# One step more between scores and transposes in the attention loop of two mix phases

## The chip, the cores and the metric

The kernel runs on one core of a Trainium2 chip. The metric is the device time of one execution in microseconds, the median over the runs of a kernel. A profiled execution has a time of its own; its trace is counted from its own start.

## The reference

The reference is two blocks of two layers each on one sequence of 512 tokens with 1024 features. The change is in the first block, in the softmax attention of both of its layers (4 heads, 96 query and key features, causal):

```python
def attend_block(args):
    qi, bi = args
    s = jnp.einsum('bqhd,bkhd->bhqk', qi, k).astype(jnp.float32) * scale
    qpos = bi * Q_BLOCK + jnp.arange(Q_BLOCK)
    causal = kpos[None, :] <= qpos[:, None]
    s = jnp.where(causal[None, None], s, jnp.finfo(jnp.float32).min)
    p = jax.nn.softmax(s, axis=-1)
    return jnp.einsum('bhqk,bkhd->bqhd', p.astype(v.dtype), v)
```

Its result stands beside two other mixers of the layer, a gate (`sgu_mixer`, products of `w_spatial` with the value half) and a pool (`pool_mixer`, running means over 2, 4, 8 and 16 tokens, then a product with `w_pool`). All three are normalized, joined and multiplied by `w_out`. Everything else, the feed-forward layers, the convolution, the second attention and the other products with large weights, is not touched.

## The kernel before, in words

Each engine has one hand-written program; the engines meet only in semaphores, and each carries out its instructions in the order written. The large products run on TensorE (PE) in weight slabs of 1 MB. The sync engine loads a slab, GpSimd (POOL) splits it into a high and a low part (L407, L411), and TensorE multiplies three times (L469 to L471). Where a phase streams slabs, TensorE is the engine that all others follow.

A mix phase (function `mix` in each engine's program, two phases, one for each layer) ends with an attention loop that is short of such products. It has 16 steps r = 0 to 15: head r // 4, block r % 4 of 128 query tokens. Because of the causal mask step r works on 128, 256, 384 or 512 keys (its width). The stages of a step are:

- scores(r), TensorE, L806, into PSUM bank 4 or 5;
- mask(r), VectorE (DVE), L1688: adds the mask, takes the row maximum, writes the buffer `W[:, r % 3]` (named work), and then L1691, the bias for the exponential. In the trace mask is an instruction and a read of its accumulator;
- exp(r), ScalarE (ACT), L1191, in place, with the row sum;
- scale(r), VectorE, L1699 and L1700: the reciprocal of the sum and the product with it, in place;
- transposes(r), TensorE, L819: one block of 128 for each 128 keys, into bank 6 or 7;
- copy(r), ScalarE, L1200: out of PSUM into `pt1` (named probs_t).

After the four steps of head h TensorE makes values(h), L790, with the transposed probabilities as moving operand, and ScalarE copies the result out, here called head copy(h), L1223. All engines count one loop variable t. In iteration t TensorE makes scores(t), then whatever stands in `between[t]`, then transposes(t-2). VectorE makes mask(t), `between[t]`, scale(t-1). ScalarE makes exp(t), copy(t-2), `between[t]`.

The `between` pieces belong to the gate and the pool, and to weight tiles of the phase. They hang on t. On TensorE: input tiles at t = 1 and 2 (24 large matmuls each), gate products at 5 (L768), pool products at 11 (L779), token sums at 13 and 15 (L508). On VectorE: pool_input at 2 and 3 (L1630), the gate at 6 and 7 (L1634, L1637), gate_sum at 9 (L1332, L1335), pool_sum at 14. On ScalarE: gate squares at 8, at 12 the copies of the pool products out of PSUM (L1177, pool_scaled) and their squares, and at t = 16 the two square roots for the token norms (L987), ahead of which a table load stands. GpSimd in the same stretch splits a slab and then computes the running means of the pool (L437 to L449).

Behind the loop TensorE makes two `spread_norm` (L516) with norms that VectorE prepares out of ScalarE's square roots, then values(3), then the first products with `w_out` (L469). These wait for the low parts of gate and pool (L1675).

Of the kernel before, what the change touches and what calls it, by code (L numbers as in the profile page):

```python
# [28 lines left out]
ACT = mybir.ActivationFunctionType  # L29
ALU = mybir.AluOpType  # L30


P = 128
T = 512
# [14 lines left out]
TOK = T // P  # L49
# [106 lines left out]
def build(nc, a):  # L156

    ctx = ExitStack()
    with ctx:
# [18 lines left out]
        ident = sb("ident", [P, P])  # L178
        ones = sb("ones", [P, P])
        cols = sb("cols_sb", [P, N_COLUMNS])  # L180
        stat = sb("stat", [P, 24])
# [12 lines left out]
        with ExitStack() as s:  # L194
# [18 lines left out]
            diag = sb("diag_sb", [P, T], F32, s)  # L213
            pa = sb("window_a", [P, T + 16], F32, s)
            pb = sb("window_b", [P, T + 16], F32, s)
            nar = sb("token_cols", [P, 232], F32, s)
# [30 lines left out]
        with ExitStack() as s:  # L247
            W = sb("work", [P, 8, T], F32, s)
# [9 lines left out]
        ps = ctx.enter_context(nc.psum_tensor("psum", [P, 8, T], F32))  # L258
# [51 lines left out]
        probs_turned = sem("probs_turned")  # L310
# [155 lines left out]
        def _(pe):  # L466
# [218 lines left out]
            def mix(p):  # L685
                L = p.layer
# [7 lines left out]
                for c in range(TOK):  # L694
                    if c % 2 == 0:
                        take(p, 4 + c // 2)
                    out = ps[:, 4 + c // 2, (c % 2) * 256:(c % 2) * 256 + 256]
                    for k in range(8):
                        ha, la = xh[:, k, c * P:(c + 1) * P], xl[:, k, c * P:(c + 1) * P]
                        hb, lb = wh[:, s, k * 256:(k + 1) * 256], wl[:, s, k * 256:(k + 1) * 256]  # L700
                        last = triple(out, ha, la, hb, lb, k == 0, k == 7)
# [10 lines left out]
                for h in range(HEADS):  # L712
                    take(p, h % 2)
                    for kk in range(2):
                        last = triple(ps[:, h % 2, :], *blk(s, 2 * h + kk), lath[:, kk, :], latl[:, kk, :], kk == 0, kk == 1)
# [78 lines left out]


                steps = HEADS * TOK
                for t in range(steps + 2):
                    if t < steps:
                        h, i = divmod(t, TOK)
                        b = 4 + t % 2  # L800
                        if i == 0:
                            pe.wait_ge(head_ready, L * HEADS + h + 1)
                            fed = 7 - h % 2
                            pe.wait_ge(drained[fed], p.drain[fed] + (2 if fed == 7 else 4) + h // 2)
                        take(p, b)
                        pe.matmul(ps[:, b, 0:(i + 1) * P], qk1[0:QK_HEAD, 2 * h, i * P:(i + 1) * P],  # L806
                                  qk1[0:QK_HEAD, 2 * h + 1, 0:(i + 1) * P], start=True, stop=True).then_inc(scores_done, 1)
                    if t > TOK + 1 and t % TOK == 2:
                        values(t // TOK - 1)
                    if t in between:  # L810
                        between[t]()
                    if t >= 2:
                        r = t - 2
                        h, i = divmod(r, TOK)
                        b = 6 + r % 2
                        pe.wait_ge(probs_ready, L * steps + r + 1)
                        take(p, b)
                        for kb in range(i + 1):
                            last = pe.transpose(ps[:, b, kb * P:(kb + 1) * P], W[:, r % 3, kb * P:(kb + 1) * P], ident[:])  # L819
                        last.then_inc(probs_turned, 1)  # L820
                spread_norm(p, 2)
                spread_norm(p, 3)
# [14 lines left out]
                for m in range(4):  # L837
                    j = 6 + m // 2
                    for k in range(4):
                        if m == 0:  # L840
                            pe.wait_ge(split_low, split_base_mix(p) + 7 + k + 1)
                        last = triple(ps[:, m, :], *blk((s0 + j) % 2, 2 * k + m % 2), mix_high[k], mix_low[k], False, k == 3)
# [103 lines left out]
        def _(act):  # L946
            step = Chain(act, act_step)
# [178 lines left out]
            def mix(p):  # L1126
                L = p.layer
# [14 lines left out]
                for c in range(TOK):  # L1142
                    if c % 2 == 0:
                        act.wait_ge(*((tile_done, p.tile + 4) if c < 2 else (slab_done, p.slab + 3)))
                    ins = act.activation(W[:, 5, 0:256], ps[:, 4 + c // 2, (c % 2) * 256:(c % 2) * 256 + 256], ACT.Square,
                                         accum_out=nar[:, 64 + c:65 + c])
# [8 lines left out]
                for n in range(2 * HEADS):  # L1155
                    part, h = divmod(n, HEADS)
                    b = 2 * part + h % 2
# [25 lines left out]
                between = {8: gate_squares, 12: pool_scaled}  # L1183

                steps = HEADS * TOK
                for t in range(steps + 2):
                    if t < steps:
                        h, i = divmod(t, TOK)
                        n = (i + 1) * P
                        act.wait_ge(max_ready, L * steps + t + 1)  # L1190
                        act.activation(W[:, t % 3, 0:n], W[:, t % 3, 0:n], ACT.Exp, scale=nar[:, 184 + t:185 + t],  # L1191
                                       bias=stat[:, t % 3:t % 3 + 1], accum_out=stat[:, 3 + t % 3:4 + t % 3]) \
                            .then_inc(exp_ready, 1)
                    if t >= 2:
                        r = t - 2
                        h, i = divmod(r, TOK)
                        act.wait_ge(probs_turned, L * steps + r + 1)
                        if i == 0:
                            at_least(act, values_done, L * HEADS + h)
                        act.activation(pt1[:, 0:i + 1, i * P:(i + 1) * P],  # L1200
                                       ps[:, 6 + r % 2, 0:(i + 1) * P].rearrange("p (k q) -> p k q", q=P), ACT.Copy) \
                            .then_inc(drained[6 + r % 2], 1)
                        if i == 1 and h >= 1:
                            o_copy(p, h - 1)
                    if t in between:
                        between[t]()
                    if t == steps:
                        token_root(2, 256)
                        token_root(3, 256)
# [110 lines left out]
        def _(dve):  # L1320
            step = Chain(dve, dve_step)
# [210 lines left out]
            def mix(p):  # L1532
                L = p.layer
                sb0 = split_base_mix(p)
                d = p.drain
                r, r2 = nar[:, 0:4], nar[:, 4:8]
# [49 lines left out]
                for c in range(TOK):  # L1586
                    b = 4 + c // 2
# [34 lines left out]
                for h in range(HEADS):  # L1622
                    b = 7 - h % 2
# [53 lines left out]
                between = {2: lambda: pool_input(0), 3: lambda: pool_input(1), 6: lambda: gate(0), 7: lambda: gate(1), 9: gate_sum, 14: pool_sum}  # L1677

                steps = HEADS * TOK
                for t in range(steps + 1):  # L1680
                    if t < steps:
                        i = t % TOK
                        n = (i + 1) * P
                        dve.wait_ge(scores_done, L * steps + t + 1)
                        if t >= 3:
                            dve.wait_ge(probs_turned, L * steps + t - 2)
                        mx = stat[:, 20 + t % 2:21 + t % 2]
                        dve.tensor_tensor_reduce(out=W[:, t % 3, 0:n], in0=ps[:, 4 + t % 2, 0:n], in1=diag[:, T - n:T], scale=1.0,  # L1688
                                                 scalar=-3e38, op0=ALU.add, op1=ALU.max, accum_out=mx).then_inc(drained[4 + t % 2], 1)
                        dve.wait_ge(drained[4 + t % 2], d[4 + t % 2] + 3 + t // 2 + 1)  # L1690
                        dve.scalar_tensor_tensor(out=stat[:, t % 3:t % 3 + 1], in0=mx, scalar=-1.0, in1=nar[:, 184 + t:185 + t],  # L1691
                                                 op0=ALU.mult, op1=ALU.mult).then_inc(max_ready, 1)
                    if t in between:
                        between[t]()
                    if t >= 1:
                        q = t - 1
                        n = (q % TOK + 1) * P
                        dve.wait_ge(exp_ready, L * steps + q + 1)
                        step(dve.reciprocal(stat[:, 22 + q % 2:23 + q % 2], stat[:, 3 + q % 3:4 + q % 3]))  # L1699
                        dve.tensor_scalar(W[:, q % 3, 0:n], W[:, q % 3, 0:n], stat[:, 22 + q % 2:23 + q % 2], None, ALU.mult) \  # L1700
                            .then_inc(probs_ready, 1)
                state["scaled"] = DT * L
                repeat_norm(2, d[2] + 7)
# [253 lines left out]
```

## Time and profile before

| | us |
|---|---|
| median of 3 runs | 2692.8 (2691.54 to 2693.14) |
| the profiled execution, its own time | 2696.47 |
| span of its trace | 2694.7 |
| TensorE busy | 2607.5 (97%) |
| VectorE, ScalarE, GpSimd busy | 1172.4, 500.9, 1630.6 |
| mean granted TensorE clock | 0.984 of full |

Busy shares are means over all phases; the loops of the two mix phases are two short stretches near 100 to 165 us and 655 to 720 us, and there the granted clock is at its lower level (half) for some of the time. Everything behind them in the program follows them, so a microsecond lost or won at the end of a loop is one of the whole time.

### The profile page before, as it was taken

To read this page: it belongs to the slowest core of one execution; us is meant where nothing else is said; L and a number is where in the kernel's file an instruction comes from. 1 tells how busy PE (TensorE), PEld (TensorE's weight loads), DVE (VectorE), ACT (ScalarE), POOL (GpSimd) and SP (SyncE) were. 2 spreads that over 40 slices of the span, in tenths; PEclk is the share of its full clock that TensorE was granted. 3 is DMA by queue.
4 is the path that set the end of the run, shared out by engine and by line. 5 is a ranking of instruction groups with operands and counts; after the bars stand their busy time and mean duration, and the time that the engine had idled before them with its cause. 6 is when DMAs were issued, how large, how long until landed. Compare 5 with 4: busy or idle time off the path is not lost.

```text
span 2694.7 us, 31567 instructions
## 1 busy us (share of the span) xinstructions
PE 2607.5 (97%) x11906; PEld 2142.5 (80%) x11906; DVE 1172.4 (44%) x1664; ACT 500.9 (19%) x849; POOL 1630.6 (61%) x1113
## 2 busy tenths in 40 slices
PE   6889999999799999999999999999999999999997
PEld 6668888888578888888888888888788878888885
DVE  5854443036644440255540513782467155504325
ACT  3342111022421110201200103200310044100022
POOL 4626677663276666666676766676247615767763
PEclk9989999998899999999999999999999999999998
DMA  4102222231022222222232223222112202222221
GB/s 152 63 26 84 102 100 94 93 116 63 16 94 93 100 103 94 94 94 95 100 109 94 94 94 106 91 103 100 48 49 105 96 32 74 96 103 94 94 95 62
DMA packets 36892, 236.71 MB, mean 88 GB/s; under 512 B 4048, under 2 KB 5584, under 8 KB 9168
## 3 DMA queue, kind: packets, MB, share of 16 engines
q1 hardware_dynamic: 33456, 230.78, 24.5%
q10 hardware_dynamic: 3360, 4.85, 0.6%
q8 instruction: 56, 0.92, 0.1%
q14 instruction: 20, 0.16, 0.0%
HBM read 233.51 MB, written 2.10 MB: 87 GB/s over the span
## 4 chain that ended last, share of the span: by engine, by line
PE 93%; DVE 3%; ACT 1%; issue 1%; POOL 0%; DMA 0%; DVEq 0%; SPq 0%; POOLq 0%; ACTq 0%
PE psum L469 29%; PE psum L471 29%; PE psum L470 29%; PE psum L918 2%; PE psum L902 1%; PE psum L680 1%; PE psum L927 1%; PE psum L790 0%; PE psum L806 0%; DVE work L1335 0%; DMA x_res<-in_x 0%; PE psum L499 0%; POOL w_low L411 0%; PE psum L752 0%; DVE stat L1691 0%
## 5 line engine op out<-in xcount | busy, mean ns | idle before, releaser
L411 POOL TENSOR_TENSOR w_low<-w_stage,w_high 128x512 fp32r<-128x512 f32 x864 | 1183.5, 1401 | 18.0
L407 POOL TENSOR_SCALAR w_high<-w_stage 128x2048 fp32r<-128x2048 f32 x216 | 416.0, 1926 | 1008.7 <-PE psum L471 996.8
L469 PE MATMUL psum<-x_high,w_high 128*128 128x512 f32 x1664 | 654.0, 393 | 18.2 <-DVE x_low L1351 18.2
L470 PE MATMUL psum<-x_low,w_high 128*128 128x512 f32 x1664 | 649.1, 390 | 0.0
L471 PE MATMUL psum<-x_high,w_low 128*128 128x512 f32 x1664 | 648.8, 390 | 0.0
L469 PEld LDWEIGHTS psum<-x_high,w_high 128*128 128x128 f32 x1664 | 313.4, 188 | 86.5 <-issue 17.7
L470 PEld LDWEIGHTS psum<-x_low,w_high 128*128 128x128 f32 x1664 | 313.3, 188 | 67.1 <-issue 2.2
L471 PEld LDWEIGHTS psum<-x_high,w_low 128*128 128x128 f32 x1664 | 313.3, 188 | 65.5
L1392 DVE TENSOR_TENSOR psum<-psum,x_res 128x512 f32<-128x512 f32 x56 | 39.2, 700 | 434.2 <-PE psum L471 431.2
L469 PE MATMUL psum<-mlp_high,w_high 128*128 (+1 forms) x576 | 224.1, 389 | 0.0
L470 PE MATMUL psum<-mlp_low,w_high 128*128 (+1 forms) x576 | 224.1, 389 | 0.0
L471 PE MATMUL psum<-mlp_high,w_low 128*128 (+1 forms) x576 | 224.1, 389 | 0.0
L469 PE MATMUL psum<-attn_x_high,w_high 128*128 128x512 f32 x384 | 150.0, 391 | 0.0
L471 PE MATMUL psum<-attn_x_high,w_low 128*128 128x512 f32 x384 | 149.4, 389 | 0.0
L470 PE MATMUL psum<-attn_x_low,w_high 128*128 128x512 f32 x384 | 149.4, 389 | 0.0
L469 PE MATMUL psum<-ffn_high,w_high 128*128 (+1 forms) x352 | 136.9, 389 | 0.0
L470 PE MATMUL psum<-ffn_low,w_high 128*128 (+1 forms) x352 | 136.9, 389 | 0.0
L471 PE MATMUL psum<-ffn_high,w_low 128*128 (+1 forms) x352 | 136.9, 389 | 0.0
L470 PEld LDWEIGHTS psum<-mlp_low,w_high 128*128 128x128 f32 x576 | 108.1, 188 | 22.6
L471 PEld LDWEIGHTS psum<-mlp_high,w_low 128*128 128x128 f32 x576 | 108.1, 188 | 22.4
L469 PEld LDWEIGHTS psum<-mlp_high,w_high 128*128 128x128 f32 x576 | 108.1, 188 | 22.4
L1055 ACT ACTIVATE mlp_high<-work 128x512 f32 x64 | 40.5, 633 | 457.0 <-DVE work L1438 457.0
(268 smaller groups left out, 3483.1 us busy)
## 6 DMA issues: line engine op xcount, KB each, us to landing
w_stage<-in_wstream SPq DMA_DIRECT2D x216, 1024.0 KB, 4.9
x_res<-in_x SPq DMA_DIRECT2D x2, 1024.0 KB, 12.4
out_x<-attn_out SPq DMA_DIRECT2D x8, 256.0 KB, 2.1
inv_count_sb<-in_inv_count ACTq DMA_DIRECT2D x2, 512.0 KB, 9.0
ple_proj<-in_p ACTq DMA_DIRECT2D x2, 512.0 KB, 3.8
qk<-in_mask ACTq DMA_DIRECT2D x1, 576.0 KB, 3.7
w_spat<-in_spatial ACTq DMA_DIRECT2D x2, 256.0 KB, 5.6
diag_sb<-in_diag ACTq DMA_DIRECT2D x2, 256.0 KB, 9.4
```

What stands on the lines that cost most here:

```text
L407: pool.tensor_scalar(wh[:, s, :], stage[:, s, :], 1.0, 1.0, ALU.mult, ALU.mult).then_inc(high_written, 1)
L411: last = pool.tensor_tensor(wl[:, s, part], stage[:, s, part], wh[:, s, part].bitcast(F32), ALU.subtract)
L469: pe.matmul(out, wa, ra, start=start, stop=False)
L470: pe.matmul(out, wa, rb, start=False, stop=False)
L471: return pe.matmul(out, wb, ra, start=False, stop=stop)
L680: last = pe.matmul(ps[:, 6, at + c:at + c + 1], W[rows, n % 2, c * P:(c + 1) * P], ones[rows, 0:1], start=True, stop=True)
L902: pe.matmul(ps[:, b, :], q[0], k[0], start=True, stop=True)
L918: last = pe.matmul(ps[:, b, r * P:(r + 1) * P], v, pt2[:, (n % 2) * 768 + kb * P:(n % 2) * 768 + (kb + 1) * P], start=kb == 0, stop=kb == 5)
L927: last = pe.transpose(ps[:, 4 + kb // 4, (kb % 4) * P:(kb % 4 + 1) * P], sc2[:, n % 2, kb * P:(kb + 1) * P], ident[:])
L1055: act.activation(hh2[:, bass.ds(i * 2 + m, 1), :].rearrange("p a t -> p (a t)"), W[:, 6 + m, :], ACT.Copy).then_inc(hidden_high, 1)
L1392: tt(ps[:, m, :], ps[:, m, :], x[:, m, :], ALU.add).then_inc(x_summed, 1)
```

## The change

The steps are taken apart by one more iteration: transposes and copy of step t-3, scale of step t-2, in four buffers of `W` in place of three. The loops get one iteration more. values(h) moves from t = 4h + 6 to t = 4h + 7, so that it still stands in front of transposes(4h + 4). The `between` pieces keep their t. The fourth buffer is `W[:, 3]`, and the column for the row sums moves from `stat[:, 3 + t % 3]` to `stat[:, 4 + t % 4]`.

```diff
@@ TensorE, mix
-                for t in range(steps + 2):
+                for t in range(steps + 3):
...
-                    if t > TOK + 1 and t % TOK == 2:
+                    if t > TOK + 2 and t % TOK == 3:
                         values(t // TOK - 1)
                     if t in between:
                         between[t]()
-                    if t >= 2:
-                        r = t - 2
+                    if t >= 3:
+                        r = t - 3
...
-                            last = pe.transpose(ps[:, b, kb * P:(kb + 1) * P], W[:, r % 3, kb * P:(kb + 1) * P], ident[:])
+                            last = pe.transpose(ps[:, b, kb * P:(kb + 1) * P], W[:, r % 4, kb * P:(kb + 1) * P], ident[:])
@@ ScalarE, mix
-                for t in range(steps + 2):
+                for t in range(steps + 3):
...
-                    if t >= 2:
-                        r = t - 2
+                    if t >= 3:
+                        r = t - 3
@@ VectorE, mix
-                for t in range(steps + 1):
+                for t in range(steps + 2):
...
-                        if t >= 3:
-                            dve.wait_ge(probs_turned, L * steps + t - 2)
+                        if t >= 4:
+                            dve.wait_ge(probs_turned, L * steps + t - 3)
...
-                    if t >= 1:
-                        q = t - 1
+                    if t >= 2:
+                        q = t - 2
```

**VectorE in iteration 9, layer 0.** Before, the rows from mask(9) on: gate_sum (L1332, L1335), then scale(8), 128 wide, then mask(10).

```order
130 L1688 ISA work,stat<-psum,diag_sb 128x256
131 L1688 ISA stat 128x1
132 L1691 SCALAR_TENSOR_TENSOR stat<-stat,token_cols 128x1
133 L1332 COPY work<-work 128x512
134 L1335 TENSOR_TENSOR work<-work 128x512
135 L1699 RECIPROCAL stat<-stat 128x1
136 L1700 TENSOR_SCALAR work<-work,stat 128x128
137 L1688 ISA work,stat<-psum,diag_sb 128x384
```

Now, in the same iteration:

```order
128 L1688 ISA work,stat<-psum,diag_sb 128x256
129 L1688 ISA stat 128x1
130 L1691 SCALAR_TENSOR_TENSOR stat<-stat,token_cols 128x1
131 L1332 COPY work<-work 128x512
132 L1335 TENSOR_TENSOR work<-work 128x512
133 L1699 RECIPROCAL stat<-stat 128x1
134 L1700 TENSOR_SCALAR work<-work,stat 128x512
135 L1688 ISA work,stat<-psum,diag_sb 128x384
```

Behind the same mask and the same gate_sum stands scale(7), 512 wide, the last step of head 1. It used to be ahead of mask(9).

**TensorE from transposes(7) to scores(12), layer 0.** Before, values(1) (four rows of L790) comes after scores(10), and the pool products (L779) after scores(11).

```order
371 L819 MATMUL psum<-ident,work 128x128 x4
372 L806 MATMUL psum<-qk 128x384
373 L790 MATMUL psum<-probs_t,v_tok 128x512
374 L790 MATMUL psum<-probs_t,v_tok 128x384
375 L790 MATMUL psum<-probs_t,v_tok 128x256
376 L790 MATMUL psum<-probs_t,v_tok 128x128
377 L819 MATMUL psum<-ident,work 128x128
378 L806 MATMUL psum<-qk 128x512
379 L779 MATMUL psum<-pool_in,w_pool_sb 64x512 x4
380 L819 MATMUL psum<-ident,work 128x128 x2
381 L806 MATMUL psum<-qk 128x128
```

Now:

```order
372 L819 MATMUL psum<-ident,work 128x128 x4
373 L806 MATMUL psum<-qk 128x512
374 L790 MATMUL psum<-probs_t,v_tok 128x512
375 L790 MATMUL psum<-probs_t,v_tok 128x384
376 L790 MATMUL psum<-probs_t,v_tok 128x256
377 L790 MATMUL psum<-probs_t,v_tok 128x128
378 L779 MATMUL psum<-pool_in,w_pool_sb 64x512 x4
379 L819 MATMUL psum<-ident,work 128x128
380 L806 MATMUL psum<-qk 128x128
```

Between transposes(7) and values(1) now stands scores(11), and values(1) and the pool products follow each other with nothing between them.

**ScalarE at the end of the loop, layer 0.** Before, from exp(15) on: copy(13), head copy(2), copy(14), then the table load and the roots, copy(15), three squares.

```order
97 L1191 ACTIVATE work,stat<-work,stat,token_cols 128x512
98 L1200 ACTIVATE probs_t<-psum 128x2x128
99 L1223 ACTIVATE mla_out<-psum 128x512
100 L1200 ACTIVATE probs_t<-psum 128x3x128
101 L987 ACT_TABLE_LOAD
102 L987 ACTIVATE token_cols<-psum,cols_sb 128x4 x2
103 L1200 ACTIVATE probs_t<-psum 128x4x128
104 L963 ACTIVATE work<-mla_out 128x512 x3
```

Now:

```order
96 L1191 ACTIVATE work,stat<-work,stat,token_cols 128x512
97 L1200 ACTIVATE probs_t<-psum 128x128
98 L1200 ACTIVATE probs_t<-psum 128x2x128
99 L1223 ACTIVATE mla_out<-psum 128x512
100 L987 ACT_TABLE_LOAD
101 L987 ACTIVATE token_cols<-psum,cols_sb 128x4 x2
102 L1200 ACTIVATE probs_t<-psum 128x3x128
103 L1200 ACTIVATE probs_t<-psum 128x4x128
104 L963 ACTIVATE work<-mla_out 128x512 x3
```

copy(14) moved from the front of the table load to behind the roots, ahead of the three squares; copy(12) is now behind exp(15).

## Rows read from the trace of the kernel before

**Rows 1.** The page: busy time of each engine over the span.

```profile
PE 2607.5 (97%) x11906; PEld 2142.5 (80%) x11906; DVE 1172.4 (44%) x1664; ACT 500.9 (19%) x849; POOL 1630.6 (61%) x1113
```

**Rows 2.** Stretches: PE, PEld, DVE, ACT, POOL busy; then granted clock, DMA.

```profile
668.49:692.50 24.01, 15.65 (x81) 9.26 (x80) 22.22 (x43) 9.49 (x25) 22.67 (x19) 0.86 0.14 44
114.02:137.70 23.68, 15.55 (x76) 9.93 (x75) 21.97 (x42) 9.34 (x24) 21.75 (x19) 0.73 0.13 44
...
701.00:705.00 4.00, 3.52 (x7) 1.50 (x6) 2.19 (x7) 1.60 (x5) 0.00 (x0) 0.62 0.00 0
```

**Rows 3.** Waits, 668.6 to 692.5: us in total, times, longest.

```profile
PE psum L819 <- DVE work L1700: 7.5, 4, 3.5
...
DVE work L1688 <- PE psum L806: 4.6, 1, 4.6
```

**Rows 4.** Timeline, layer 1, VectorE: scales, gate_sum, mask(10); start, duration.

```profile
686.69 1.50 DVE L1700 TENSOR_SCALAR work<-work,stat 128x512 f32<-128x512 f32 x1
...
689.80 1.57 DVE L1335 TENSOR_TENSOR work<-work 128x512 f32<-128x512 f32 x1
...
691.48 1.09 DVE L1700 TENSOR_SCALAR work<-work,stat 128x128 f32<-128x128 f32 x1
692.50 0.55 DVE L1688 CUSTOM_DVE_ANT_0 work<-psum,diag_sb 128x384 f32<-128x384 f32 x1
...
697.64 0.49 DVE L1700 TENSOR_SCALAR work<-work,stat 128x512 f32<-128x512 f32 x1
```

**Rows 5.** Timeline, layer 1, GpSimd.

```profile
686.64 1.26 POOL L446 TENSOR_TENSOR window_b<-window_a 64x512 f32<-64x512 f32 x1
...
690.90 1.59 POOL L449 TENSOR_TENSOR pool_in<-window_a,pool_in 128x512 f32<-128x512 f32 x1
```

**Rows 6.** Timeline, layer 1, TensorE, from values(1) to scores(12).

```profile
690.62 2.96 PE L790 MATMUL psum<-probs_t,v_tok 128*128 128x512 f32 x8
...
693.52 1.02 PE L806 MATMUL psum<-qk 96*128 96x512 f32 x2
694.48 1.93 PE L779 MATMUL psum<-pool_in,w_pool_sb 64*64 64x512 f32 x8
...
696.62 0.39 PE L806 MATMUL psum<-qk 96*128 96x128 f32 x2
```

**Rows 7.** Timeline, layer 1, ScalarE: exp and copy.

```profile
693.28 0.71 ACT L1191 ACTIVATE work<-work,stat,token_cols 128x384 f32<-128x384 f32 x1 [2.71 <-DVE stat L1691]
...
697.10 0.59 ACT L1223 ACTIVATE mla_out<-psum 128x512 f32<-128x512 f32 x1
...
698.06 0.48 ACT L1200 ACTIVATE probs_t<-psum 128x384 f32<-128x384 f32 x1
```

**Rows 8.** Timeline, layer 1, TensorE and ScalarE, the end of the loop.

```profile
701.85 4.12 PE L790 MATMUL psum<-probs_t,v_tok 128*128 128x512 f32 x8 [0.48 <-ACT probs_t L1200]
...
709.97 1.28 ACT L987 ACT_TABLE_LOAD   x1
...
720.30 0.50 PE L469 MATMUL psum<-gate_pool_high,w_high 128*128 128x512 f32 x1 [2.21 <-DVE gate_pool_low L1675]
```

**Rows 9.** Timeline, layer 0: values(1), scores(12), values(2), table load, first output product.

```profile
136.65 3.46 PE L790 MATMUL psum<-probs_t,v_tok 128*128 128x512 f32 x8
...
143.15 0.39 PE L806 MATMUL psum<-qk 96*128 96x128 f32 x2
...
148.38 2.42 PE L790 MATMUL psum<-probs_t,v_tok 128*128 128x512 f32 x8 [0.48 <-ACT probs_t L1200]
...
154.80 1.28 ACT L987 ACT_TABLE_LOAD   x1
...
165.13 0.50 PE L469 MATMUL psum<-gate_pool_high,w_high 128*128 128x512 f32 x1 [1.12 <-DVE gate_pool_low L1675]
```

**Rows 10.** Waits, 696 to 712, the end of the loop of layer 1.

```profile
DVE work L1688 <- PE psum L806: 6.6, 3, 3.2
...
DVE stat L1699 <- ACT work L1191: 0.4, 1, 0.4
```

More of the change, by code:

```diff
@@ L1190, in mix @@
                         act.wait_ge(max_ready, L * steps + t + 1)
-                        act.activation(W[:, t % 3, 0:n], W[:, t % 3, 0:n], ACT.Exp, scale=nar[:, 184 + t:185 + t],
-                                       bias=stat[:, t % 3:t % 3 + 1], accum_out=stat[:, 3 + t % 3:4 + t % 3]) \
+                        act.activation(W[:, t % 4, 0:n], W[:, t % 4, 0:n], ACT.Exp, scale=nar[:, 184 + t:185 + t],
+                                       bias=stat[:, t % 4:t % 4 + 1], accum_out=stat[:, 4 + t % 4:5 + t % 4]) \
                             .then_inc(exp_ready, 1)
-                    if t >= 2:
-                        r = t - 2
+                    if t >= 3:
+                        r = t - 3
                         h, i = divmod(r, TOK)
@@ L1684, in mix @@
                         dve.wait_ge(scores_done, L * steps + t + 1)
-                        if t >= 3:
-                            dve.wait_ge(probs_turned, L * steps + t - 2)
+                        if t >= 4:
+                            dve.wait_ge(probs_turned, L * steps + t - 3)
                         mx = stat[:, 20 + t % 2:21 + t % 2]
-                        dve.tensor_tensor_reduce(out=W[:, t % 3, 0:n], in0=ps[:, 4 + t % 2, 0:n], in1=diag[:, T - n:T], scale=1.0,
+                        dve.tensor_tensor_reduce(out=W[:, t % 4, 0:n], in0=ps[:, 4 + t % 2, 0:n], in1=diag[:, T - n:T], scale=1.0,
                                                  scalar=-3e38, op0=ALU.add, op1=ALU.max, accum_out=mx).then_inc(drained[4 + t % 2], 1)
                         dve.wait_ge(drained[4 + t % 2], d[4 + t % 2] + 3 + t // 2 + 1)
-                        dve.scalar_tensor_tensor(out=stat[:, t % 3:t % 3 + 1], in0=mx, scalar=-1.0, in1=nar[:, 184 + t:185 + t],
+                        dve.scalar_tensor_tensor(out=stat[:, t % 4:t % 4 + 1], in0=mx, scalar=-1.0, in1=nar[:, 184 + t:185 + t],
                                                  op0=ALU.mult, op1=ALU.mult).then_inc(max_ready, 1)
@@ L1694, in mix @@
                         between[t]()
-                    if t >= 1:
-                        q = t - 1
+                    if t >= 2:
+                        q = t - 2
                         n = (q % TOK + 1) * P
                         dve.wait_ge(exp_ready, L * steps + q + 1)
-                        step(dve.reciprocal(stat[:, 22 + q % 2:23 + q % 2], stat[:, 3 + q % 3:4 + q % 3]))
-                        dve.tensor_scalar(W[:, q % 3, 0:n], W[:, q % 3, 0:n], stat[:, 22 + q % 2:23 + q % 2], None, ALU.mult) \
+                        step(dve.reciprocal(stat[:, 22 + q % 2:23 + q % 2], stat[:, 4 + q % 4:5 + q % 4]))
+                        dve.tensor_scalar(W[:, q % 4, 0:n], W[:, q % 4, 0:n], stat[:, 22 + q % 2:23 + q % 2], None, ALU.mult) \
                             .then_inc(probs_ready, 1)
```

## The prediction

> **What bounds the kernel now.** I read the page first: TensorE is busy 97% of the span, VectorE 44% [rows 1]. These are means over many phases, and the change touches none of the large products, so I went on to the two loops. In the stretches of time for the first part of the loop, from scores(3) to the end of scale(8), VectorE is busy 22.22 of 24.01 us in layer 1 and 21.97 of 23.68 in layer 0, TensorE only 15.65 and 15.55 [rows 2]. The list of waits says the same: there TensorE waits for scale four times, 7.5 us in all, and VectorE waits for scores only once, 4.6 us, which is the input tile ahead of mask(3) [rows 3]. So up to iteration 9 the loop is as long as VectorE's list of instructions.
>
> It is long because of GpSimd. A scale of 512 takes 0.49 us when GpSimd is idle, and 1.50 us at 686.69; it ends at 688.19, just 0.29 after GpSimd's instruction of 686.64 ends at 687.90 [rows 4, 5]. GpSimd is busy 22.67 of the 24.01 us [rows 2]. Its last instruction in the loop ends at 692.49 [rows 5].
>
> From iteration 10 on the bound changes. TensorE has values(1), scores(11), the pool products, and then the three engines wait for each other in turn: VectorE waits 6.6 us for scores from 696 on [rows 10].
>
> **The change, part by part.** Nothing is added or removed; every instruction is there as before, and one iteration more in each loop. What matters is what stands behind what.
>
> *What the deeper order takes away.* scale(t-1) could wait for exp(t-1); scale(t-2) can't. In the end of the loop of layer 1 VectorE waits for exp once, 0.4 us [rows 10], and in the first part there is no such wait. TensorE's wait for scale is not loosened: it still makes in iteration t what VectorE scaled in iteration t-1. I take the gain as 0.4 us for each layer at most; it lies in the end, which step C counts as a whole.
>
> The Trainium skill speaks for the change at this point: "Perfetto Trace Analysis", section "Optimization Strategy", says that a gap which repeats on the engine that should be saturated can mean too few buffers. By that rule the four waits of TensorE, 7.5 us, are what a fourth buffer could give back, up to 15 us over the two layers and 2678 in all. The rows speak against it: the engine waited for has 22.22 of 24.01 us of work of its own.
>
> *Step B, iterations 3 to 12.* VectorE's list up to the end of iteration 9 is the same, but each scale is one step older: scale(1) to scale(7) in place of scale(2) to scale(8). The last, behind gate_sum, is now 512 wide, not 128. In layer 1 it ends 0.29 after GpSimd's last instruction, at 692.8, where scale(8) ended at 692.57 [rows 4, 5]. So far 0.2 us. But before, values(1) ran from 690.62 on, under gate_sum and scale(8), and scores(11) was issued at 693.52 [rows 6]. Now transposes(7) wait for that late scale(7), and values(1) needs copy(7), which needs transposes(7). In layer 1: transposes(7) from 692.8, some 0.45 for four blocks (estimate: the pool products and two blocks of transposes take 2.14 from 694.48 to 696.62, of which 1.93 is the products' own row), scores(11) 0.96 (693.52 to 694.48), done 694.2. copy(7) also stands behind exp(10): mask(10) from 692.7, exp 0.78 later (692.50 to 693.28 before), 0.71 for exp, 0.6 for a copy of 512 (estimate from 0.48 for 384) [rows 4, 6, 7]. That is 694.8. values(1) at the full clock 2.3 (a little under the 2.42 of the row in layer 0), pool products 1.9: scores(12) at 699.1, where it was at 696.62 [rows 6, 9]. **2.5 us later.** values(1) is no longer hidden.
>
> In layer 0 the same chain starts at 137.7, when mask(10) could start (end of the stretch in rows 2): copy(7) done 140.0, values(1) to 142.3, scores(12) at 144.3 instead of 143.15: 1.2 us. It is less because values(1) was late there anyway, 136.65 and 3.46 long, at the lower clock [rows 9]. If it still is at the lower clock, add 1.0; transposes(7) and scores(11) at the lower clock add up to 0.6 in either layer. The granted clock of that stretch was 0.73 in layer 0 and 0.86 in layer 1 [rows 2], so I take 1.9 for layer 0 (1.2 to 2.6) and 2.7 for layer 1 (2.5 to 3.1).
>
> *Step C, from scores(12) to the table load.* Before 11.65 us in layer 0 and 13.35 in layer 1 (696.62 to 709.97) [rows 6, 8, 9]. Three things change. (1) Ahead of the copies of the pool products ScalarE has copy(9) and head copy(1), 0.59, in place of copy(10), 0.48 [rows 7]: about +0.5. (2) values(2) stands behind scores(15), and its copy(11) behind exp(14), which waits for scores(14). From token sum to values(2) I lay 0.8 token sum, 0.3 transposes(10), 0.65 scores(14), 0.2 on the way, 0.78 mask to exp, 0.7 exp, 0.6 copy: 4.1, where it was 2.7 (estimates scaled by width from rows 4, 6 and 7): +1.4. (3) From values(2) to the table load it was 6.4 (148.38 to 154.80), since scores(15), mask(15), exp(15), a head copy and copy(14) followed one by one; now mask(15) and exp(15) run under values(2), and behind it come token sum, transposes(13), copy(13), head copy(2): 2.3 + 0.8 + 0.3 + 0.6 + 0.6 = 4.6. That is -1.8. In sum +0.1 to +0.2. In layer 1 values(2) took 4.12, at a granted clock of 0.62 over 701 to 705 [rows 2, 8], against 2.42 in layer 0 [rows 9]; at the full clock it would win 1.6 there, and in either layer it can cost 1.6 at the lower one. Before, TensorE had waited much ahead of it, and it still will. I take one of two as slow: +1.0 for layer 0 (0.2 to 1.8), -0.7 for layer 1 (-1.5 to +0.1).
>
> *Step D, from the table load to the first output product.* 10.33 us in both layers (154.80 to 165.13, 709.97 to 720.30), although the clocks differed: this is a chain on ScalarE and VectorE [rows 8, 9]. Now copy(14), 0.48 [rows 7], stands in it, ahead of the squares that VectorE adds up. +0.5 in each layer (0.4 to 0.6).
>
> *Costed at nothing.* The fill: values(0) moves too, but under VectorE's saturated list [rows 2]. GpSimd's windows end before the pool products, which now come later. Everything behind the loop follows TensorE one to one.
>
> **Sum.** Layer 0: 1.9 + 1.0 + 0.5 = 3.4. Layer 1: 2.7 - 0.7 + 0.5 = 2.5. Together 5.9 us, bounds 1.2 + 0.2 + 0.4 + 2.5 - 1.5 + 0.4 = 3.2 and 2.6 + 1.8 + 0.6 + 3.1 + 0.1 + 0.6 = 8.8. The profiled execution took 2696.47 with a span of 2694.7; the runs' median is 2692.8. The stretches are the same program's, and the difference of 3.7 is 0.14% and not in them, so I add to the median: **2698.7**, own range 2696.0 to 2701.6. A measurement of this kernel can tell 0.2% (5.4 us) from nothing, and the forecast lies right at it.
>
> **The rivals.**
>
> *It washes out.* values(1) may be exposed by less: if VectorE's list up to iteration 9 gets shorter by 1 us or more, because the scales meet GpSimd's instructions differently (each such meeting moves an end by up to 1 us, 0.49 against 1.50 [rows 4]), B halves. With B at 1.0 and 1.3, C at its lower bounds and D at 0.5 the sum is 2.0: 2694.8. Against it: VectorE has gate_sum and seven scales there all the same, and the number of meetings does not fall.
>
> *Faster.* scores now stands one step ahead of values, so VectorE has work during values(1) and values(2), and 6.6 us of its waiting in layer 1's end alone [rows 10] could be given back. This decides if B stays under about 0.5 us, that is if copy(7) is ready when scores(11) is done. Then a layer wins what (3) of step C wins, 1.8, the exp wait of 0.4 and, in layer 1, 1.6 of clock, less 0.5 for D: 1.7 and 3.3, 2687.8. Against it: copy(7) can't be ahead of a scale(7) that ends behind gate_sum, and (1) and (2) of step C take the same time back.
>
> *Worse.* TensorE waits longer ahead of values(1), and the lower clock holds on: all of values(1), the pool products (another 1.9) and values(2) at half rate in both layers. 8.8 plus 1.5 to 4: about 2704. For it: the clock of 0.73 and 0.62 in such stretches [rows 2]. Against it: values(1) and the pool products now follow each other without a gap, and in layer 0 the engine was already back at full clock for values(2), 2.42 us [rows 9].
>
> **How the numbers follow.** Forecast (3.2 to 8.8 later): 0.60, of it 0.40 beyond 5.4 us. Washes out: 0.22. Faster: 0.08. Worse: 0.10. So slower by over 0.2%: 0.50; within: 0.42; faster: 0.08. The range goes from 2694.0, which leaves out the faster case and the lowest part of the second, to 2702.5, which takes in the upper bound and a third of the worst case.
>
> **What would show it.** B: in iteration 10 transposes(7) right behind a 512 wide scale that ends with or behind gate_sum; values(1) starting 3 to 4 us later than before and the pool products directly behind it; scores(12) 1.2 to 3 us later, counted from scores(3). C: mask(15) and exp(15) under values(2), 4.6 us from values(2) to the table load. D: copy(14) and copy(15) between roots and squares, and about 10.8 from table load to L469. It would be wrong if scores(12) came no later, or if VectorE's stretch up to mask(10) changed by more than 1 us.

## The result, and the profile after

The changed kernel is slower: ratio 1.0026 to the kernel before, 95% interval 1.0017 to 1.0035. The medians of ten runs each are 2703.16 us (2697.21 to 2709.56) and 2694.76 us (2691.54 to 2698.36). By the ratio that is 7.0 us (4.6 to 9.4), and the medians differ by 8.4; forecast were 5.9. The median itself, 2703.16, lies above the range of 2694.0 to 2702.5: the forecast was added to 2692.8, the median of three runs of the kernel before, and that of ten is 2.0 higher. In the experiments below two single runs, 3312 us of e6 and 4099 us of e8, were in a much slower state and are left out of every median and ratio.

The two profiled executions differ much less, 2696.9 against 2694.7 us of span; the changed kernel's took 2698.68 us in its own time and was the third fastest of its ten. To see why, the span is cut at four points that both traces have: scores(0) and the first output product of each layer. The rows are the stretches outside the loops, as the windows view has them, first of the kernel before, then of the changed one; columns as in [rows 2].

```profile
0.00:100.82 100.82, 79.82 (x423) 68.44 (x423) 64.41 (x98) 37.52 (x64) 49.11 (x38) 0.95 0.35 123
165.13:656.15 491.02, 488.02 (x2216) 405.30 (x2217) 186.17 (x220) 94.75 (x152) 301.42 (x208) 0.98 0.26 91
720.30:2694.70 1974.40, 1941.05 (x8820) 1601.97 (x8820) 833.41 (x1134) 310.35 (x496) 1227.64 (x825) 0.99 0.25 89
```

```profile
0.00:98.99 98.99, 79.14 (x423) 67.44 (x423) 64.43 (x98) 37.54 (x64) 49.30 (x38) 0.97 0.35 125
168.25:654.52 486.27, 483.24 (x2216) 401.67 (x2217) 186.10 (x220) 94.58 (x151) 301.54 (x208) 0.99 0.27 92
722.67:2696.90 1974.23, 1941.06 (x8820) 1602.58 (x8820) 833.86 (x1134) 310.52 (x497) 1227.23 (x825) 0.99 0.26 89
```

Between the two loops the same 2216 matmuls took 491.02 us in one execution and 486.27 in the other, with a granted clock of 0.98 and 0.99. Nothing there was changed. So this one execution of the changed kernel got 1.8 us back at the start, 4.8 in the middle and 0.2 at the end, and lost 4.95 and 4.00 in the two loops: 8.95 - 6.75 = 2.2. The stretches tell more about the change than the spans do, and the medians of many runs more than either span.

| stretch (us) | before, layer 0 / 1 | after, layer 0 / 1 |
|---|---|---|
| scores(0) to scores(12) | 42.33 / 40.47 | 44.63 / 44.80 |
| scores(12) to table load | 11.65 / 13.35 | 13.91 / 12.64 |
| table load to first output product | 10.33 / 10.33 | 10.72 / 10.71 |
| sum | 64.31 / 64.15 | 69.26 / 68.15 |

Layer 1, VectorE's timeline of the changed kernel around gate_sum, to be laid beside [rows 4]:

```profile
685.00 1.43 DVE L1700 TENSOR_SCALAR work<-work,stat 128x384 f32<-128x384 f32 x1
686.35 0.41 DVE L1688 CUSTOM_DVE_ANT_0 work<-psum,diag_sb 128x256 f32<-128x256 f32 x1
...
688.02 1.57 DVE L1335 TENSOR_TENSOR work<-work 128x512 f32<-128x512 f32 x1
...
689.70 1.29 DVE L1700 TENSOR_SCALAR work<-work,stat 128x512 f32<-128x512 f32 x1
690.92 0.55 DVE L1688 CUSTOM_DVE_ANT_0 work<-psum,diag_sb 128x384 f32<-128x384 f32 x1
```

Behind gate_sum stands the scale of width 512, step 7, and it ends at 690.99. From mask(3), at 667.81, to mask(10) it is 23.11 us, where it was 22.95 (669.55 to 692.50); in layer 0 the two are 23.60 and 23.50. VectorE's list got longer by no more than 0.2 us. TensorE's timeline from transposes(7) on, beside [rows 6]:

```profile
691.05 1.12 PE L819 MATMUL psum<-ident,work 128*128 128x128 f32 x4 [2.38 <-DVE work L1700]
691.96 1.92 PE L806 MATMUL psum<-qk 96*128 96x512 f32 x2
693.67 3.69 PE L790 MATMUL psum<-probs_t,v_tok 128*128 128x512 f32 x8
697.29 1.93 PE L779 MATMUL psum<-pool_in,w_pool_sb 64*64 64x512 f32 x8
...
699.32 0.39 PE L806 MATMUL psum<-qk 96*128 96x128 f32 x2
```

transposes(7) start as scale(7) ends. Then scores(11), values(1) and the pool products run without a gap, 7.2 us in which VectorE has little to do. transposes(7) and scores(11) take 1.12 and 1.92 us where they take 0.66 and 1.02 at the full clock (e9, below), and values(1) 3.69 in place of 2.42; only the pool products, 1.93, are as short as before. The stretch has a granted clock of 0.57 (first row). values(2) in layer 1 was at the full clock this time, the four microseconds ahead of it were not (second row):

```profile
690.90:697.30 6.40, 6.25 (x16) 3.47 (x16) 2.38 (x11) 2.19 (x5) 0.00 (x0) 0.57 0.01 3
703.00:707.00 4.00, 4.00 (x14) 2.54 (x13) 1.55 (x5) 2.66 (x8) 0.00 (x0) 0.57 0.00 0
```

ScalarE in the same time and at the end of the loop, beside [rows 7, 8]:

```profile
692.40 0.57 ACT L1200 ACTIVATE probs_t<-psum 128x512 f32<-128x512 f32 x1
...
711.96 1.28 ACT L987 ACT_TABLE_LOAD   x1
713.25 0.42 ACT L987 ACTIVATE token_cols<-psum,cols_sb 128x4 f32<-128x4 f32 x2
713.56 0.98 ACT L1200 ACTIVATE probs_t<-psum 128x384 f32<-128x384 f32 x2
```

copy(7) is done at 692.97, before values(1) starts at 693.67: with TensorE at the lower clock it was scores(11), not copy(7), that held values(1). The last row is copy(14) and copy(15) together behind the roots. In layer 0 the changed kernel's rows that answer to [rows 9] are

```profile
138.63 3.02 PE L790 MATMUL psum<-probs_t,v_tok 128*128 128x512 f32 x8
...
143.62 0.39 PE L806 MATMUL psum<-qk 96*128 96x128 f32 x2
...
152.52 2.91 PE L790 MATMUL psum<-probs_t,v_tok 128*128 128x512 f32 x8
...
168.25 0.50 PE L469 MATMUL psum<-gate_pool_high,w_high 128*128 128x512 f32 x1 [2.51 <-DVE gate_pool_low L1675]
```

### The profile page after: what moved, and what is told of

It is laid out like the page before. It is cut to its first block, busy times and chain, and to the rows that moved or that the text cites. A ratio compares the mean times of both kernels' runs of the same rounds, so it can differ in the third digit from the quotient of the medians.

```text
span 2696.9 us, 31565 instructions
## 1 busy us (share of the span) xinstructions
PE 2607.0 (97%) x11906; PEld 2141.8 (79%) x11906; DVE 1172.3 (43%) x1664; ACT 500.9 (19%) x849; POOL 1630.1 (60%) x1113
## 4 chain that ended last, share of the span: by engine, by line
PE 93%; DVE 4%; ACT 1%; issue 1%; POOL 0%; DMA 0%; DVEq 0%; SPq 0%; POOLq 0%; ACTq 0%
PE psum L469 29%; PE psum L470 29%; PE psum L471 29%; PE psum L918 2%; PE psum L902 1%; PE psum L680 1%; PE psum L927 1%; DVE work L1335 1%; PE psum L806 1%; PE psum L790 0%; PE psum L499 0%; DMA x_res<-in_x 0%; POOL w_low L411 0%; DVE stat L1691 0%; PE psum L752 0%
## 5 line engine op out<-in xcount | busy, mean ns | idle before, releaser
L470 PEld LDWEIGHTS psum<-x_low,w_high 128*128 128x128 f32 x1664 | 313.1, 188 | 67.1 <-issue 2.2
```

The lines of the kernel that those rows point to most:

```text
L470: pe.matmul(out, wa, rb, start=False, stop=False)
```

## The experiments

The theory after the result: the order is the cause (scale(7) behind gate_sum, values(1) and the pool products behind it, in the open), and the lower clock makes it larger. Rivals: the deeper pipeline costs as such, by its extra iteration; the clock alone is the cause; the loss needs GpSimd beside VectorE. The table has the stretches of layer 0 / layer 1 from each kernel's one profile, "both loops" as the sum of the six, and the median of its runs. In e1 and e8 the pool products stand behind scores(12) and not ahead of it, so of these two only the sums can be laid beside the other kernels. Each ratio is to runs of the kernel before on the same chip, whose medians were 2694.76 to 2695.8.

| kernel | scores(0) to (12) | to table load | to output | both loops | median | ratio to before (interval) |
|---|---|---|---|---|---|---|
| before | 42.33 / 40.47 | 11.65 / 13.35 | 10.33 / 10.33 | 128.5 | 2694.76 | 1 |
| changed | 44.63 / 44.80 | 13.91 / 12.64 | 10.72 / 10.71 | 137.4 | 2703.16 | 1.0026 (1.0017 to 1.0035) |
| e1 pieces later | 42.13 / 40.51 | 13.15 / 13.14 | 10.33 / 10.34 | 129.6 | 2694.99 | 0.9999 (0.9990 to 1.0008) |
| e2 gate_sum later | 42.45 / 42.23 | 13.92 / 13.90 | 10.72 / 10.72 | 133.9 | 2699.72 | 1.0017 (1.0007 to 1.0027) |
| e3 changed, filler | 44.28 / 44.63 | 12.69 / 12.28 | 10.72 / 10.72 | 135.3 | 2700.73 | 1.0020 (1.0011 to 1.0028) |
| e4 before, filler | 39.97 / 39.99 | 13.35 / 13.03 | 10.34 / 10.34 | 127.0 | 2688.97 | 0.9980 (0.9972 to 0.9989) |
| e5 before, no means | 38.67 / 38.68 | 12.59 / 12.59 | 10.33 / 10.33 | 123.2 | 2690.15 | 0.9977 (0.9967 to 0.9987) |
| e6 changed, no means | 38.31 / 38.33 | 13.84 / 13.85 | 10.71 / 10.71 | 125.8 | 2686.69 | 0.9968 (0.9955 to 0.9981) |
| e7 before, more filler | 39.97 / 39.98 | 11.65 / 11.66 | 10.33 / 10.33 | 123.9 | 2689.47 | 0.9981 (0.9970 to 0.9991) |
| e8 e1 with filler | 39.56 / 39.51 | 15.86 / 14.84 | 10.33 / 10.34 | 130.4 | 2692.51 | 0.9985 (0.9976 to 0.9994) |
| e9 changed, more filler | 42.96 / 42.96 | 11.70 / 11.71 | 10.72 / 10.72 | 130.8 | 2695.55 | 1.0002 (0.9994 to 1.0011) |
| e10 before, gate_sum later | 42.23 / 41.93 | 13.33 / 12.57 | 10.34 / 10.34 | 130.7 | 2696.87 | 0.9999 (0.9990 to 1.0008) |

### e1: all pieces one iteration later

```diff
-                between = {1: lambda: input_tile(2), 2: lambda: input_tile(3), 5: gate_products, 11: pool_products,
-                           13: lambda: token_sum(p, 2, 2), 15: lambda: token_sum(p, 3, 2)}
+                between = {2: lambda: input_tile(2), 3: lambda: input_tile(3), 6: gate_products, 12: pool_products,
+                           14: lambda: token_sum(p, 2, 2), 16: lambda: token_sum(p, 3, 2)}
...
-                    if t == steps:
+                    if t == steps + 1:
                         token_root(2, 256)
```

> The changed kernel with every between piece one iteration later on all engines (TensorE 2, 3, 6, 12, 14, 16; ScalarE 9, 13, the roots at 17; VectorE 3, 4, 7, 8, 10, 15), so that each piece again stands beside the same transposes, scales and copies as before the change, and only scores, mask and exp run one step ahead. Theory (the loss is the new neighbourhood: scale(7) behind gate_sum, values(1) and pool products one behind the other, the head copy ahead of the pool copies): the loss goes, scores(0) to the first output product comes back from 69.3 and 68.2 us to 63 to 66 in each layer, the time to within 4 us of the kernel before. Rival (the deeper pipeline itself costs, by one more iteration of fill and drain): it stays 4 us or more behind the kernel before. Rival (the loss is TensorE's lower clock by chance of the runs): no change against the changed kernel.

The hunk shown is TensorE's; the tables of ScalarE and VectorE move in the same way. The loss is gone: 0.9999 (0.9990 to 1.0008), and the layers take 65.6 and 64.0 us, where they took 64.3 and 64.2 before and 69.3 and 68.2 in the changed kernel. So one more iteration of fill and drain, with a fourth buffer, costs no more than about 2 us, and the pipeline, as deep as in the changed kernel, gives back no more than about 3.

### e2: gate_sum alone one iteration later

```diff
-                between = {2: lambda: pool_input(0), 3: lambda: pool_input(1), 6: lambda: gate(0), 7: lambda: gate(1), 9: gate_sum, 14: pool_sum}
+                between = {2: lambda: pool_input(0), 3: lambda: pool_input(1), 6: lambda: gate(0), 7: lambda: gate(1), 10: gate_sum, 14: pool_sum}
```

> The changed kernel with one piece moved alone: gate_sum on VectorE from t = 9 to t = 10, so that scale(7) is no longer behind it. Theory: transposes(7) and with them values(1) come 1.5 to 2 us earlier; from scores(0) to scores(12) 43.3 us in layer 1 in place of 44.8, about 1.3 us less in each layer, 2 to 3 us in all. If values(1) is late for another reason (the clock, or copy(7) behind exp(10)) scores(12) doesn't move by more than 0.5 us.

The move wins 2.2 and 2.6 us from scores(0) to scores(12), more than the 1.3 expected. Layer 1 gives 1.3 of that back behind scores(12), where the token sum, scores(15) and values(2) took 1.68, 1.91 and 2.83 us in place of 1.05, 1.40 and 2.42 (the clock again), and the two loops win 3.5. The medians differ by 3.4 as well, but the intervals of the two ratios overlap, so that the whole time alone would not show it. The rows of layer 1, VectorE and then TensorE:

```profile
690.11 1.50 DVE L1700 TENSOR_SCALAR work<-work,stat 128x512 f32<-128x512 f32 x1
691.53 0.55 DVE L1688 CUSTOM_DVE_ANT_0 work<-psum,diag_sb 128x384 f32<-128x384 f32 x1
...
693.20 0.69 DVE L1335 TENSOR_TENSOR work<-work 128x512 f32<-128x512 f32 x1
```

```profile
691.66 1.11 PE L819 MATMUL psum<-ident,work 128*128 128x128 f32 x4 [0.59 <-DVE work L1700]
692.57 1.91 PE L806 MATMUL psum<-qk 96*128 96x512 f32 x2
694.27 2.95 PE L790 MATMUL psum<-probs_t,v_tok 128*128 128x512 f32 x8
```

transposes(7) start 34.71 us behind scores(0), which is at 656.95 there, in place of 36.53: 1.8 less. Another 0.7 is clock, values(1) taking 2.95 instead of 3.69. And gate_sum's sum is now 0.69 long in place of 1.57, since GpSimd is done by then (its last instruction ends at 692.75).

### e10: the same move in the kernel before

The edit is that of e2.

> The kernel before with gate_sum on VectorE at t = 10 in place of 9, the same move that brought the changed kernel 2.2 and 2.6 us from scores(0) to scores(12). Here values(1) is already running when gate_sum ends, so the theory expects less than 0.5 us there (42.33 and 40.47 us before, up to 1 more or less with the clock) and no difference in time. If gate_sum's place matters by itself, whatever the depth, it wins 2 us in each layer.

Ratio 0.9999. Layer 0 moves by 0.1 us from scores(0) to scores(12). Layer 1 is 1.5 us longer, and there values(1) took 4.41 us in place of 2.96 [rows 6], at the lower clock. The move wins nothing here, though each stretch carries such a term of clock. So the place of gate_sum matters where it stands ahead of the scale that values(1) needs, and not by itself.

### e3 and e4: filler, to take the clock out

```diff
+                        take(p, b)
+                        if t in (4, 7, 8, 9, 10):
+                            for _ in range(10):
+                                pe.transpose(ps[:, b, 0:P], ident[:], ident[:])
                         pe.wait_ge(probs_ready, L * steps + r + 1)
-                        take(p, b)
```

(e4: on the kernel before, `t in (4, 7, 8, 9)`.)

> The changed kernel with ten more transposes of the identity, into the PSUM bank that the real transposes then overwrite, ahead of the wait for scale in iterations 4, 7, 8, 9 and 10 of both loops: extra work in time in which TensorE idles. It tells how much of the loss is the lower clock. If the clock is a large part: the granted clock from scores(0) to scores(12) rises from 0.85 to 0.95 or more, values(1) falls from 3.69 (layer 1) to 2.4 us, and each layer wins 1 to 2 us, 2 to 4 in all. If the order alone is the cause, no gain, or a loss of up to 1 us for each layer, since the filler of iteration 10 can stand in the way of transposes(7).

> The kernel before with the same filler in iterations 4, 7, 8 and 9. In layer 0 values(1) ran at the lower clock there (3.3 us). If the clock matters as much in the kernel before as in the changed one, layer 0 wins 1 to 1.5 us, layer 1 up to 1.5 (values(2) is not covered by it), 1 to 3 us in all; if it is only the changed kernel that pays for the clock, less than 1 us.

More work for TensorE made the loops of both kernels shorter in their profiles, and e4 is the fastest kernel so far, 0.9980. In layer 0 of e4 scores(12) comes 2.4 us earlier than before. But 1.7 us of that are lost again behind it, because values(2), which this filler does not cover, was at the lower clock:

```profile
147.04 4.12 PE L790 MATMUL psum<-probs_t,v_tok 128*128 128x512 f32 x8 [0.48 <-ACT probs_t L1203]
```

e3 fell short: the granted clock of its stretch rose to 0.96, but values(1) was again slow, 3.76 us in layer 0 and 4.12 in layer 1. TensorE still waited 2.31 us ahead of transposes(7), behind the filler; e9 fills this wait as well. The ratio of e3, 1.0020, can't be told from the 1.0026 of the changed kernel.

### e7 and e9: both kernels with the waits filled

e7 is e4 and, at the end of iteration 12, 16 more transposes of the identity into the bank of the next real ones. e9 has the same (and 28 in place of 10 in iteration 10, the wait for scale(7)) on the changed kernel.

```diff
                         last.then_inc(probs_turned, 1)
+                        if t == 12:
+                            at_least(pe, drained[7], p.drain[7] + used[7])
+                            for _ in range(16):
+                                pe.transpose(ps[:, 7, 0:P], ident[:], ident[:])
```

> The kernel before with the filler of iterations 4, 7, 8 and 9 and 16 more transposes of the identity at the end of iteration 12, where TensorE waits for the copies of the pool products ahead of the token sum. If values(2), 3.9 us at the lower clock, is then at the full clock, the stretch from scores(12) to the table load falls from 13.0 to 13.4 us to 11.7, 1.4 us in each layer, and the time by 2 to 3 us below the 2689.0 of the kernel with less filler. If the lower clock there is not set by this wait, no change.

> The changed kernel with filler that covers TensorE's waits as in the fuller of the two fillers of the kernel before: ten transposes in iterations 4, 7, 8 and 9, 28 in iteration 10 (the wait for scale(7)), 16 at the end of iteration 12. With it TensorE should be at the full clock for values(1), the pool products and values(2) in both kernels, so their difference is the order's alone. If steps B, C and D as predicted for the full clock are right: scores(0) to scores(12) 2.5 to 3 us longer than 39.97, scores(12) to the table load 0.2 longer than 11.65, the rest 0.4 longer than 10.33; together about 3.3 us for each layer. If the clock was the whole cause, less than 1 us for each layer. If most of the loss was in the order beyond my terms, more than 4.

These two give the cleanest comparison. Both layers of each kernel now agree within 0.02 us, and values(1) and values(2) take 2.42 us in both. The filler of e9 is not on the path: TensorE still waits 0.36 us behind it, for scale(7), which ends at 690.11.

```profile
688.78 1.33 DVE L1707 TENSOR_SCALAR work<-work,stat 128x512 f32<-128x512 f32 x1
```

```profile
690.17 0.66 PE L822 MATMUL psum<-ident,work 128*128 128x128 f32 x4 [0.36 <-DVE work L1707]
```

For layer 1 the stretch from scores(0) to scores(12) by the windows view, first of e7, then of e9, and values(1) in the timelines of e7 and e9:

```profile
646.79:686.77 39.98, 35.43 (x194) 25.14 (x193) 30.27 (x68) 13.45 (x36) 26.37 (x22) 0.96 0.15 53
```

```profile
653.57:696.53 42.96, 37.13 (x219) 27.14 (x218) 29.87 (x66) 13.05 (x35) 26.21 (x22) 1.00 0.14 50
```

```profile
681.30 2.42 PE L790 MATMUL psum<-probs_t,v_tok 128*128 128x512 f32 x8
```

```profile
692.15 2.42 PE L790 MATMUL psum<-probs_t,v_tok 128*128 128x512 f32 x8 [0.46 <-ACT probs_t L1207]
```

The granted clock of layer 1 is 0.96 in e7 and not 1.00, and transposes(7) and scores(10) took 1.11 and 1.49 us there, at the lower clock. In layer 0, where it is 1.00, the stretch is as long, 39.97, so this lay off the path. The order costs 42.96 - 39.97 = 2.99, 11.70 - 11.65 = 0.05 and 10.72 - 10.33 = 0.39: 3.4 us for each layer, 6.8 in all. The medians differ by 6.1; they are from two chips, and by the ratios it is 5.7. At the full clock values(1) waits 0.46 us for copy(7), as step B had it. e7 did not get below e4 in time, though its loops are 3.1 us shorter in the profiles; that part of the expectation missed. One profile of e4 need not be typical of it, and 0.0001 between the ratios is far inside the intervals.

### e5 and e6: without GpSimd's running means

The function `windows` is left out but for one small memset for each tile that gives its signal, so the pool product multiplies unprocessed tiles.

```diff
-                    chain(tt(pa[:, 1:n], pin[:, f, 1:n], pin[:, f, 0:n - 1], ALU.add))
...
-                    tt(pin[:, f, 16:], pa[:, 16:n], pin[:, f, 16:], ALU.subtract).then_inc(pool_ready, 1)
+                    pool.memset(pin[:, f, 0:16], 0.0).then_inc(pool_ready, 1)
```

> The kernel before without GpSimd's running means (its instructions at L437 to L449 but for one small memset for each tile; the pool product then multiplies the unprocessed tiles). GpSimd has no work beside iterations 5 to 10. Theory: VectorE's list there was long because of GpSimd; from mask(3) to mask(10) it falls from 23.0 us to 17 to 19, and the loop with it, 3 to 5 us for each layer. Rival: the stretch is VectorE's own work, and nothing changes by more than 1 us.

> The changed kernel without the same running means. If the loss is the order of the pieces (values(1) behind scale(7) behind gate_sum), it stays whatever GpSimd does: from scores(0) to the first output product 3 to 5 us longer in each layer than the kernel before without means. If it needs GpSimd's contention (late scales of full width), the two kernels without means are within 1.5 us of each other in each layer. If the deeper order only needed a VectorE that isn't full, it is now faster than the kernel before without means.

From mask(3) to mask(10) it is now 17.5 us in e5 and 17.7 in e6, in place of 23.0 and 23.1: 5.5 us of VectorE's list were GpSimd's. The loops of e5 got shorter by only 2.7 and 2.6 us, where 3 to 5 were expected. The loss by the order falls to 1.3 us for each layer (62.88 - 61.60), all of it behind scores(12); up to there e6 is 0.4 us shorter. Taken as it stands, that is the case of the expectation in which the loss needs GpSimd. But the clock confounds this: values(1), layer 1, of e5 and of e6 (L778 there is L790 in the other kernels):

```profile
684.00 4.63 PE L778 MATMUL psum<-probs_t,v_tok 128*128 128x512 f32 x8 [0.32 <-ACT probs_t L1188]
```

```profile
678.97 2.64 PE L778 MATMUL psum<-probs_t,v_tok 128*128 128x512 f32 x8
```

With 2.0 us of clock taken off e5, the order would cost e6 about 1.6 us before scores(12) where it costs 3.0 with the means. So about half of step B needs GpSimd, by this estimate; no run here has both kernels without the means at the full clock. In the medians e6 is 3.5 us ahead of e5, with overlapping intervals, although its loops are 2.6 us longer; the rest of the program made that difference, and which part of it is chance stays open.

### e8: e1 with filler

The filler of e3 in iterations 5, 8, 9, 10 and 11, on top of e1.

> The changed kernel with all pieces one iteration later and filler in iterations 5, 8, 9, 10 and 11. If what the filler wins is independent of the depth, it comes to 2689 to 2690, like the kernel before with filler. If the step ahead of scores helps once the clock holds, it is 2 us or more below that; if one more iteration costs, above 2692.

It gave 2692.5, above the 2692 that was named as the sign of a cost, and its loops are 0.8 us longer than those of e1. Behind scores(12) it took 15.86 and 14.84 us, where e1 took 13.15 and 13.14: values(2), which has no filler ahead of it, was at the lower clock, 3.88 and 4.12 us in place of e1's 2.42. In layer 1:

```profile
703.23 4.12 PE L790 MATMUL psum<-probs_t,v_tok 128*128 128x512 f32 x8 [0.38 <-ACT probs_t L1203]
```

One of the five places was a poor choice besides: the filler of iteration 11 comes between values(1) and scores(12), on the path, where it takes some 1.1 us. So this run does not settle whether a step more helps once the clock holds; it only found no sign of it.

## Why the prediction was right

**What bounds the kernel.** Right. VectorE's list from mask(3) to mask(10) kept its length (23.0 and 23.1 us), and e5 shows 5.5 us of it to be GpSimd's.

**The gain, taken as 0.4 us for each layer at most.** It fits: e1 has the depth without the order and lies at 0.9999. A gain of 0.4 is too small for its interval to show. The rule of the Trainium skill in "Perfetto Trace Analysis", section "Optimization Strategy", did not hold here. TensorE's waits for scale in the same stretch were 7.5 us [rows 3] and are 8.0 with a fourth buffer, by the list of waits of the changed kernel from 668 to 691:

```profile
PE psum L819 <- DVE work L1700: 8.0, 4, 3.2
```

They come from the work of the engine waited for, which was busy 22.22 of 24.01 us [rows 2]. The rule says "can mean", and the busy share of the other engine is what tells it apart.

**Step B** forecast 1.9 and 2.7 us; it is 2.30 and 4.33. The mechanism is as forecast: scale(7) directly behind gate_sum, transposes(7) with its end, values(1) later than before by 3.8 us in layer 0 (counted from scores(0), 35.83 to 39.64) and 4.7 in layer 1 (34.47 to 39.15), the pool products directly behind. At equal clock it is 2.99 in both layers (e9 less e7); the term for layer 1 at the full clock was 2.5. The 1.2 of layer 0 was counted against a kernel before whose values(1) was slow, so the figure beside it is e9 less the kernel before, 42.96 - 42.33 = 0.6. The mis-sized term in layer 1 is the clock. Transposes(7) and scores(11) at the lower clock were put at up to 0.6 more, and they made values(1) start 0.6 later than in e9. That values(1) could be slow too was left out of the bound of 3.1; it took 3.69 in place of 2.42, 1.3 more. So layer 1 lies outside its range, and so does the sign that scores(12) comes 1.2 to 3 us later, counted from scores(3): it is 2.4 in layer 0 and 4.4 in layer 1.

**Step C** forecast +1.0 and -0.7; it is +2.26 and -0.71. At equal clock it is 0.05, forecast 0.1 to 0.2, and its three parts are there in e9 less the kernel before, layer 0: scores(12) to the token sum +0.4 (forecast +0.5), on to values(2) +1.6 (+1.4), on to the table load -1.9 (-1.8). What the sum left out is the clock ahead of values(2): the token sum, scores(14) and scores(15) took 1.60, 1.49 and 1.91 us in layer 0, in place of 1.05, 0.81 and 1.02 in e9, while only values(2) was counted, hence 2.26, above the bound of 1.8. That layer 1 came out as forecast is luck. values(2) was at the full clock there, for which the forecast's own bound was -1.5, and the slow instructions ahead of it (scores(14) 1.49 us) took 0.9 of that back.

**Step D** forecast 0.5 in each layer (0.4 to 0.6); it is 0.39 and 0.38. The cost is gone in e1, where copy(14) is again ahead of the roots.

**Sum.** The loops of the profiled execution lost 8.95 us where 5.9 were forecast (upper bound 8.8); the time lost 7.0 by the ratio (4.6 to 9.4) and 8.4 by the medians, within the 3.2 to 8.8. At equal clock the order costs 6.8. By the forecast's own terms at the full clock, 2.5, 0.2 and 0.5, each layer would lose 3.2 us, and it is 3.4. So the order was sized about right, and the clock in the changed kernel took more than was allowed for it.

**The rivals.** Faster: its condition, step B under 0.5 us, was met up to scores(12) in layer 0 of e2 (0.1 us more than before) and in e6 against e5, there by way of the clock. The loops did not get shorter for it: layer 0 of e2 took 67.1 us where it took 64.3 before, and each loop of e6 was 1.3 us longer than e5's. Washing out did not happen in the changed kernel, but it is what e1 is.

## What to carry to other kernels

To deepen one chain of a software pipeline moves everything that hangs on the same loop variable against that chain. List, for each stage, which foreign pieces are now ahead of it, and ask for whom it was on time. If the depth must change, move the pieces along (e1), and first look whether the engine that is waited for is idle at all; here it was full, and there was nothing to win. And look at what a wait of TensorE does to the matmuls behind it: work of no use, put into the waits, made this kernel faster by 0.2% (e4, 2688.97 us), the best here of the versions that compute the whole result, with e7 (2689.47) level with it.

## What the runs showed of the hardware

Filler paid, by 6.0 us in the median and 5.4 by the ratio (3.0 to 7.5), though it adds 40 transposes to each loop. It was not expected to be more than 3. By the profiles the loops account for 1.5 us of it. Between the loops, where nothing was changed, e4 needed 483.14 us at a granted clock of 1.00, the kernel before 491.02 at 0.98:

```profile
165.49:648.63 483.14, 480.13 (x2216) 399.47 (x2217) 185.38 (x220) 94.59 (x151) 302.54 (x208) 1.00 0.26 92
```

Whether the filler has a hand in that stays open, and the other profiles give no sign of it: with filler this stretch took 487.9 us (e3), 484.8 (e7), 488.0 (e8) and 487.7 (e9), without it 486.3 (changed, e2, e10), 489.4 (e1), 487.9 (e5) and 483.2 (e6, granted clock 1.00). What the rows do show is that a stretch of the same instructions differs by 8 us between executions whose granted clocks differ, as much as the whole effect studied here.
